# One paired input product in place of two chunks, and row scales spread by a transpose of a repeated column

## What is computed

```python
# first stack, 2 layers: four mixers side by side on one projection
for l in range(2):
    h = rms_norm(x, mix_norm_g[l])
    proj = h @ w_in[l]             # 1024 -> 2660 columns
    moba_p, mla_p, sb_p, ssm_p = split(proj, (768, 352, 768, 772))
    # mla_p: 192 columns cq, 128 ckv, 32 kr; the last 4 of ssm_p are dt
    x = x + concat(moba, mla, stick_breaking, mamba2) @ w_out[l]
    h = rms_norm(x, ffn_norm_g[l])
    u = causal_dwconv(h @ ffn_w_in[l], ffn_conv_w[l]) + ffn_conv_b[l]
    x = x + (silu(gate) * up) @ ffn_w_out[l]
# second stack, 4 layers: half a swiglu, a mixer (a, b, c, a), half a swiglu
```

## Time and profile before

| | |
|---|---|
| median of 3 runs | 2599.91 us (2598.31 to 2601.88) |
| the profiled execution | 2599.22 us, its span 2597.3 us |
| TensorE busy | 2562.4 us, 99% of the span |
| VectorE, ScalarE, GpSimd busy | 65%, 51%, 6% |
| mean granted TensorE clock | 0.998 of full |

### The profile page before, as it was taken

The page is one execution under the profiler, slowest core; times in us unless marked ns, Lnnn a source line. Parts: engine busy times, 40 slices in busy tenths (PEclk is TensorE's granted clock), DMA queues, the critical chain, the costliest instruction groups (busy, mean ns, idle before and its releaser), DMA issues.

```text
span 2597.3 us, 43244 instructions
## 1 busy us (share of the span) xinstructions
PE 2562.4 (99%) x18462; PEld 2378.8 (92%) x18462; DVE 1688.5 (65%) x2364; ACT 1322.2 (51%) x1938; POOL 156.9 (6%) x228
## 2 busy tenths in 40 slices
PE   8999999999999999999999999999999999999998
PEld 7999899998998989989988998998899899897997
DVE  6878567785665766656656665666766566566663
ACT  6756466654544554444455444444554454355542
POOL 2100011000000000000011000002000000000000
PEclk9999999999999999999999999999999999999999
DMA  7267552665766547567664766665457567563863
GB/s 223 86 175 215 170 160 84 181 193 162 209 189 200 181 134 198 184 182 195 187 218 139 198 192 178 192 190 192 147 152 198 185 179 196 191 207 99 219 186 122
DMA packets 568313, 460.26 MB, mean 177 GB/s; under 512 B 12346, under 2 KB 529290, under 8 KB 568122
## 3 DMA queue, kind: packets, MB, share of 16 engines
q1 hardware_dynamic: 562615, 441.91, 58.0%
q0 software_dynamic: 4656, 15.30, 1.8%
q10 hardware_dynamic: 851, 0.28, 0.0%
HBM read 456.37 MB, written 1.10 MB: 176 GB/s over the span
## 4 chain that ended last, share of the span: by engine, by line
PE 90%; DVE 5%; ACT 3%; DMA 1%; issue 1%; POOL 0%; DVEq 0%; POOLq 0%; SPq 0%; ACTq 0%
PE ps L899 28%; PE ps L764 16%; PE ps L766 16%; PE ps L765 16%; PE ps L718 3%; PE ps L720 3%; PE ps L719 3%; DVE wlo L1882 1%; ACT h_hi L1303 1%; DMA raw<-in_w_in 1%; PE ps L643 1%; DVE h_lo L1943 1%; ACT prob L1303 1%; ACT whi L1303 1%; PE ps L1001 1%
## 5 line engine op out<-in xcount | busy, mean ns | idle before, releaser
L1882 DVE TENSOR_TENSOR wlo<-raw,whi 128x2048 fp32r<-128x2048 f32 (+1 forms) x419 | 956.6, 2285 | 499.9 <-ACT whi L1303 499.2
L1303 ACT ACTIVATE whi<-raw 128x2048 fp32r<-128x2048 f32 (+1 forms) x421 | 802.9, 1910 | 793.2 <-DMA raw<-in_ff_w_in 420.2
L764 PE MATMUL ps<-h_hi,whi 128*128 128x256 f32 x3584 | 1006.9, 281 | 0.0
L765 PE MATMUL ps<-h_lo,whi 128*128 128x256 f32 x3584 | 1003.3, 280 | 0.0
L766 PE MATMUL ps<-h_hi,wlo 128*128 128x256 f32 x3584 | 1003.0, 280 | 0.0
L764 PEld LDWEIGHTS ps<-h_hi,whi 128*128 128x128 f32 x3584 | 673.7, 188 | 5.0 <-issue 5.0
L766 PEld LDWEIGHTS ps<-h_hi,wlo 128*128 128x128 f32 x3584 | 674.9, 188 | 0.0
L765 PEld LDWEIGHTS ps<-h_lo,whi 128*128 128x128 f32 x3584 | 673.4, 188 | 0.0
L899 PE MATMUL ps<-whi,hid_lo 128*128 128x512 f32 x880 | 296.2, 396 | 0.0
L899 PE MATMUL ps<-whi,hid_hi 128*128 128x512 f32 x880 | 295.2, 394 | 0.0
L899 PE MATMUL ps<-wlo,hid_hi 128*128 128x512 f32 x880 | 294.5, 394 | 0.0
(11 more groups left out here) (312 smaller groups left out, 2135.5 us busy)
## 6 DMA issues: line engine op xcount, KB each, us to landing
raw<-in_ff_w_in SPq DMA_DIRECT2D x176, 1024.0 KB, 6.1
raw<-in_ff_w_out SPq DMA_DIRECT2D x88, 1024.0 KB, 5.0
raw<-in_ffn_w_in SPq DMA_DIRECT2D x44, 1024.0 KB, 6.0
raw<-in_a_w_qkv SPq DMA_DIRECT2D x24, 1024.0 KB, 5.2
raw<-in_ffn_w_out SPq DMA_DIRECT2D x22, 1024.0 KB, 4.9
raw<-in_w_in SPq DMA_DIRECT2D x19, 1024.0 KB, 5.3
raw<-in_c_w_qkv SPq DMA_DIRECT2D x12, 1024.0 KB, 5.1
raw<-in_w_out SPq DMA_DIRECT2D x8, 1024.0 KB, 4.9
```

Of the source, the lines that this page charges most:

```text
L764: e.matmul(out, hi, m.h_hi[:, k, :], start=(k == 0), stop=False)
L765: e.matmul(out, hi, m.h_lo[:, k, :], start=False, stop=False)
L1303: return self.nc.scalar.activation(*a, **k)
L1882: self.e.tensor_tensor(chunk_view(m.wlo[:, slot, :], c), chunk_view(m.raw[:, slot, :], c), chunk_view(m.whi[:, slot, :], c).bitcast(F32), ...
```

## The change

It does four things.

1. The 356 columns of chunks 0 and 1 are cut into two chunks of 178, and `pair` multiplies both at once: a matmul has 356 moving columns, from two slots of the ring, and writes one bank for each `t` (banks 2 and 3). It needs both chunks before it starts and reports both done at its end. The eviction is one ScalarE instruction for each `t`.
2. Chunks 2 and 3 no longer wait for an eviction, as their banks 0 and 1 are free. In layer 0 they wait for `rows_kept`, since `turn_rows` now writes banks 0 and 1, between the two token tiles of the pair.
3. In layer 0 the first halves of both chunks are loaded and split before the start; the transfer of the four dt columns is the third on ScalarE's queue, the transfer of the tables goes behind chunk 3, and GpSimd makes `rs` before it issues its 13 transfers.
4. `spread` transposes `rs[:, t]` repeated over 128 columns, and `diagonals` is gone.

```diff
+PAIR = (QR + KVR + ROPE + 4) // 2
+IN_PIECES = ((C_CQ, [(C_CQ, PAIR)]), (C_CQ + PAIR, [(C_CQ + PAIR, PAIR - 4), (W_DT, 4)]),
...
     def spread(self):
...
-        e.wait_ge(s.diagonals, TT * r)
+        e.wait_ge(s.rstd, TT * self.rounds["norm"])
         for t in range(TT):
-            ins = e.matmul(m.ps[:, 3, t * P:(t + 1) * P], m.ones, m.diag[:, t, :], start=True, stop=True)
+            ins = e.transpose(m.ps[:, 3, t * P:(t + 1) * P], m.rs[:, t:t + 1].to_broadcast([P, P]), m.ident)
...
+    def pair(self, turn=None):
...
+        self.at(s.bank_free, self.b0)
+        if c == 0:
+            e.wait_ge(s.first_lo, 1)
+        else:
+            e.wait_ge(s.split_lo, c + 2)
+        for t in range(TT):
+            out = view(m.ps[:, 2 + t, 0:2 * PAIR], a=2)
+            for k in range(KT):
+                if k % 4 == 0:
+                    self.wait_features(2 * t + k // 4 + 1)
+                if (c, t, k) == (0, 0, 4):
+                    e.wait_ge(s.split_lo, 2)
+                if turn is not None and (t, k) == (0, 6):
+                    turn()
...
+            if t == 0:
+                ins.then_inc(s.pair_half, 1)
+                if turn is None:
+                    self.turn_rows()
+        ins.then_inc(s.chunk_done, 2)
...
+        self.paired = True
         if r == 1:
             self.begin_product()
-            chunk(0)
-            self.turn_rows()
-            chunk(1)
+            self.pair()
+            e.wait_ge(s.rows_kept, 1)
         chunk(2)
         chunk(3)
...
     def mix(self, l):
...
-        self.split(0, 0)
+        if l > 0:
+            self.split(0, 0)
         e.wait_ge(s.rstd, TT * self.rounds["norm"])
-        keep(0)
+        keep_tile(0)
+        if l == 0:
+            self.split(0, 0)
         self.split(1, 0)
-        keep(1)
-        self.split(2, 0)
+        keep_tile(1)
         e.wait_ge(s.bank_free, self.b0 + 2)
         self.act(m.c_squares, proj[:, :, C_CQ:C_KR], ACT.Square).then_inc(s.c_sq, 1)
+        self.split(2, 0)
...
     def first_norm(self, gain):
-        self.e.wait_ge(self.s.params_in, 16)
+        e, m, s, d = self.e, self.m, self.s, self.d
+        e.wait_ge(s.params_in, 16)
         for t in range(TT):
             self.rstd_x(t)
+        e.wait_ge(s.landed[1], 16 * landings(1))
+        e.dma_start(m.ext[:, 0:2 * REL + 1], d.a_rel_bias.rearrange("l h c -> (l h) c")).then_inc(s.ext_in, 16)
+        self.layer_rows(0)
```

More of the change, by code:

```diff
@@ L393 @@
     gates_ring = False
+    paired = False
     a0 = 0
@@ L539, in pick @@
             return to, of
-        for b in range(1 if l == 0 else 0, IN_CHUNKS):
+        for b in range(2 if l == 0 else 0, IN_CHUNKS):
             self.chunk(b, 0, pick)
-            if l == 0 and b == 1:
+            if l == 0 and b == 3:
                 e.dma_start(m.consts[:, CONST["upto"][0]:], d.consts[:, CONST["upto"][0]:CONST["dist"][0]]).then_inc(s.tables_in, 16)
@@ L669, in turn_rows @@
         for r in range(ROW_TILES):
-            ins = e.transpose(m.ps[:, 2 + r // 4, (r % 4) * P:(r % 4 + 1) * P], m.rows[:, r, :], m.ident)
+            ins = e.transpose(m.ps[:, r // 4, (r % 4) * P:(r % 4 + 1) * P], m.rows[:, r, :], m.ident)
         ins.then_inc(s.rows_turned, 1)
@@ L729, in tokens_chunk @@
         self.last.then_inc(self.s.chunk_done, 1)
+    def pair(self, turn=None):
+        e, m, s = self.e, self.m, self.s
+        c = self.c0
+        whi, wlo = (a[:, c % SLOTS:c % SLOTS + 2, :].rearrange("p s (k c) -> p k s c", k=KT) for a in (m.whi, m.wlo))
+        self.at(s.bank_free, self.b0)
[3 more added lines that the diff above has]
+            e.wait_ge(s.split_lo, c + 2)
+        for t in range(TT):
+            out = view(m.ps[:, 2 + t, 0:2 * PAIR], a=2)
[6 more added lines that the diff above has]
+                    turn()
+                hi, lo = m.h_hi[:, k, t * P:(t + 1) * P], m.h_lo[:, k, t * P:(t + 1) * P]
+                w_hi, w_lo = whi[:, k, :, 0:PAIR], wlo[:, k, :, 0:PAIR]
+                e.matmul(out, hi, w_hi, start=(k == 0), stop=False)
+                e.matmul(out, hi, w_lo, start=False, stop=False)
+                ins = e.matmul(out, lo, w_hi, start=False, stop=(k == KT - 1))
+            if t == 0:
[3 more added lines that the diff above has]
+        ins.then_inc(s.chunk_done, 2)
     def head(self, turn, kind):
         gates = kind in ("swiglu", "ffn1")
-        widths = IN_WIDTH[0:HEAD] if kind == "mix1" else [256] * HEAD
         self.begin_product()
+        if kind == "mix1":
+            self.pair(turn)
+            return
         for t in range(TT):
@@ L1335, in split_first @@
         m, s = self.m, self.s
-        self.e.wait_ge((s.first_landed, s.landed[0])[half], 16)
-        part = slice(1024 * half, 1024 * half + 1024)
-        self.act(m.whi[:, 0, part], m.raw[:, 0, part], ACT.Copy).then_inc((s.first_hi, s.split_hi)[half], 1)
+        if half == 0:
+            self.e.wait_ge(s.first_landed, 48)
+        else:
+            self.e.wait_ge(s.landed[0], 16)
+            self.e.wait_ge(s.landed[1], 16)
+        for b in range(2):
+            ins = self.act(first_half(m.whi, b, half), first_half(m.raw, b, half), ACT.Copy)
+        ins.then_inc((s.first_hi, s.split_hi)[half], 1 + half)
     def square_x(self, t):
@@ L1955, in first_norm @@
         self.turn_lo(1, gain)
-        for b in range(1 - AHEAD, 0):
-            self.split(b, 0)
+        self.split(2 - AHEAD, 0)
         self.e.wait_ge(self.s.rows_kept, 1)
@@ L1963, in split_first @@
         self.e.wait_ge((s.first_hi, s.split_hi)[half], 1)
-        part = slice(1024 * half, 1024 * half + 1024)
-        self.e.tensor_tensor(m.wlo[:, 0, part], m.raw[:, 0, part], m.whi[:, 0, part].bitcast(F32),
-                             ALU.subtract).then_inc((s.first_lo, s.split_lo)[half], 1)
+        for b in range(2):
+            ins = self.e.tensor_tensor(first_half(m.wlo, b, half), first_half(m.raw, b, half), first_half(m.whi, b, half).bitcast(F32),
+                                       ALU.subtract)
+        ins.then_inc((s.first_lo, s.split_lo)[half], 1 + half)
     def weigh_sum(self, t, half, weight):
@@ L2913, in landings, with first_half @@
 def landings(c):
-    return sum(2 if k in NARROW else 1 for k in range(c % SLOTS, c + 1, SLOTS))
+    return sum(2 if k > 1 and k in NARROW and k - 1 in NARROW else 1 for k in range(c % SLOTS, c + 1, SLOTS))
+def first_half(a, b, half):
+    return a[:, b, :].rearrange("p (k c) -> p k c", k=KT)[:, 4 * half:4 * half + 4, 0:PAIR]
 def chunk_view(ap, c):
```

60 lines of the change are left out of this document (26 added, 34 removed).

## The result

| | before | after |
|---|---|---|
| median of the runs | 2599.86 us (8 runs, 2598.31 to 2601.88) | 2608.61 us (8 runs, 2605.38 to 2610.40) |
| profiled execution, its span | 2599.22, 2597.3 | 2605.38, 2603.5 |

The ratio is 1.0031, with an interval of 1.0021 to 1.0040: the change costs 8.7 us.

The account below looks back on a forecast made before the run. TensorE is busy 99% of the span, but chunk 5's arrival sets layer 0's time. Gains of 1.5 (layer 0), 0.8 (layer 1) and 2.4 (`spread`) sum to 4.7 us, giving 2595.2; range 2590.5 to 2601.

Parts of the forecast that it names:

- Price of a matmul: Mixers' input product: one 356-column matmul takes 0.163 us in place of a pair's 0.230, saving 3.2 us of TensorE per layer.
- Layer 1: 0.8 us: Layer 1's input product: wait in the pair 1.2 us, stand of 1.8 before `cn`, gain 0.8 of the 3.2 us.
- the bound with the fallen clock: Layer 1: a loss of 1.3 us if the clock falls after its stand as after the longer one.
- Layer 0, start: Start of layer 0: larger first loads, small dt pieces and splits move the first matmul from 10.19 to 13.0.
- Layer 0, chunk 5: Layer 0's weight transfer: slot freed at 23.0, landing at 29.6, transposes of `cn` at 37.4.
- second rival: Layer 0: GpSimd's 13 transfers meet chunks 4 and 5; with the old 15.57 us, landing 38.6, time 2604.2; chance 0.1.
- Layer 0, TensorE: Before layer 0's `cn`: TensorE arrives at 34.3, stands 3.1 us, loses 2.1 to low clock; layer 0 gains 1.5.
- The clock: TensorE behind layer 0's stand: a 2.4 us stand lowered the clock, 1.45 did not, so 2.1 us is counted.
- `spread`: 2.4 us: In 11 places two transposes of 0.22 us replace four passes of 0.44, a 2.4 us gain; lost VectorE work counts nothing.

Follow-up runs that it names:

- experiment 2: The changed kernel with the pair only in layers after the first; layer 0's start, loads and order as before, on chunks of 178 columns: 2604.34 us.
- experiment 4: The changed kernel without the transfer of the four dt columns in 1024 small pieces, loading 178 neighbouring columns in layer 0: 2606.29 us.
- experiment 5: The changed kernel, with GpSimd waiting for chunk 5 ahead of the `up` weights and last rows, and no longer for chunk 3 between them: 2602.59 us.
- 7: The kernel before with only the new `spread`, each of its two transposes issued twice (four passes): 2602.80 us.
- experiment 1: The kernel before with only the new `spread`: two transposes of the repeated column in 11 places, no diagonal matrix: 2603.41 us, ratio 1.0019.
- 9: The kernel before with the new `spread`'s two transposes, but VectorE's diagonals still made and waited for: 2604.93 us.
- experiment 10: The kernel before with only the new `spread`, plus one extra matmul at chunk 11 of the hidden product in each `swiglu` stage: 2602.02 us.
- 3: The changed kernel, with chunk 5 split behind the chain that makes `cn` on ScalarE and VectorE, and chunk 2 evicted before it: 2602.54 us.
- 6: The changed kernel with the old `spread` (diagonal matrices, two float32 matmuls), so the pair alone: 2606.51 us.

## Why the prediction was wrong

Said: 2595.2. Came: 2608.6, outside the range. By its own steps:

- **Price of a matmul.** Said 0.163 for 356 columns, measured 0.167. Right.
- **Layer 1: 0.8 us.** Came 0.7, with a wait in the pair of 1.0 (said 1.2) and a stand of 1.7 (said 1.8). Right in mechanism and size; experiment 2 shows that the bound with the fallen clock can be met.
- **Layer 0, start.** Said 13.0 for the first matmul, came 14.94. The step priced the 1024 small pieces at 1.2 us, from a microsecond in which 845 small packets passed alone; experiment 4 measures them at 3.2. The term was mis-sized, and it moved the end of the pair from 23.0 to about 25.2.
- **Layer 0, chunk 5.** This is the step that failed. Said: landing at 29.6, from a queue that stays full behind 13.4 us. It did not stay full. Everything issued early had landed by about 23.6, and chunk 5 could not leave until 25.30, so its time was its own 5.35 us (experiment 5) plus what GpSimd's transfers took, and they had moved to exactly this place: 11.29. I had written that they "start late and leave the queue to the weights"; they left it to chunks 2 to 4, which nobody waited for, and met chunk 5. That is the second rival ("Chunk 5 is no faster than before"), to which I gave 0.1: landing 36.6 against its 34.3 to 38.6. By that rival's own formula this landing gives 2602.2; what is missing to 2608.6 is the drift and the distance of the median from the profile, both below.
- **Layer 0, TensorE.** Stand 7.8 where I said 3.1; the clock fell behind it, 2.3 us where I said 2.1. Together layer 0 lost 5.66 where I had a gain of 1.5.
- **The clock.** That it falls behind a stand of 3 us was read off two stands of before, and the runs do not bear out that the length decides. Ahead of `cn` in layer 0 the clock fell with stands of 2.24 us (experiment 2) and 2.37 (7), and held with 2.32 (1) and 2.35 (9). In experiment 10 it fell while TensorE was busy, 1.6 us before its stand for the eviction of chunk 0. That the cost came near (2.3 for 2.1) says nothing for the rule, as the stand was 7.8 us and not 3.1. What decides between holding and falling is open. The Trainium skill's rule that I weighed ("TensorE: Matmul & The Clock Gate", section "HAM oscillation — how this bites in real kernels": gaps in which TensorE waits for data bring its clock to half) agrees with the stands of 7.8, 3.2 and 2.56 us; behind those of 1.71, 2.32 and 2.35 us the granted clock stayed at 1.00. Experiment 1, the matmul behind the stand and the stretch from it on; then experiment 10, two stretches ahead of the stand and the matmul behind it:

```profile
40.68 0.33 PE L1079 MATMUL ps<-consts,xn 128*128 128x128 f32 x1 [2.32 <-DVE xn L2454]
40.68:45.00 4.32, 4.32 (x37) 4.32 (x38) 4.18 (x8) 4.00 (x7) 0.00 (x0) 1.00 0.54 187
```

```profile
20.00:21.80 1.80, 1.80 (x19) 1.80 (x17) 1.71 (x1) 0.06 (x1) 1.66 (x3) 0.99 1.00 335
21.80:23.39 1.59, 1.59 (x8) 1.42 (x7) 0.58 (x1) 1.16 (x1) 1.42 (x3) 0.50 0.97 297
25.11 0.55 PE L718 MATMUL ps<-whi,h_hi 128*128 128x256 f32 x1 [1.72 <-ACT proj L1308]
```

- **`spread`: 2.4 us.** The places gave 2.5, and the step stopped there. That two passes fewer change the rate at which the 19 chunks behind run was in none of my terms or rivals; I put it at nothing without a reason, and with it the part costs 4.2 us (experiment 1). This is the second step that failed. The rate of 5.71 is in no row of before, but its trace already had two rates, seven stages at 5.65 and one at 5.62, and a gain of 0.22 stood ahead of 912 matmuls, where 1% more on each is 1.0.

The median lies 3.2 us above the profiled execution of after. Three more stages at 5.71 would do it (five of the eight were not at it in that profile, and experiments 1, 2, 3 and 5 show five or six that are), but the slower executions have no trace, so this is argued and not shown. A stand with a fallen clock in a later mixer, as in the profile of 6 (4.4 us), would do it too.

Open is what sets the rate. The steps of matmuls repeat every six, and the first ones behind the `spread` already differ; that is all that the traces show. The Trainium skill says in "TensorE: Matmul & The Clock Gate", section "Architectural detail: the array is 16× 32×32, not 1× 128×128", that TensorE's queue may pull weight loads ahead of matmuls in flight; whether that is what locks in differently, no run here shows.

## What to carry to other kernels

Before a transfer is moved later, ask what its issue waits for and what is in the queue at that moment, not how full the queue is on average: a full queue ahead of it hides the wait for its slot, an empty one doesn't. Where a chain of small results stands behind a large piece of work that it does not need, in two engines' queues, move it ahead first; a saving on TensorE ahead of such a chain is easily lost (here the pair in layer 1 cost 0.9 us with the chain behind chunk 5, and gained 2.6 by the profiles with the chain ahead). And when a change of a few passes stands ahead of a long run of equal matmuls, compare the period of that run in both traces: 1% of it was more than four times the gain.

## What the hardware showed that I had not expected

- A run of equal matmuls (128 x 256, float32r) on TensorE ran here at one of three steady rates at the full granted clock: 5.62, 5.65 and 5.71 us for 48 of them. It kept the one in which it entered, over 912 matmuls, and one matmul more moved it from 5.71 to 5.65 in mid-run, in five stages of five.
- 1024 pieces of 16 bytes, in one transfer beside others, delayed the first matmul by 3.2 us, nearly three times the 1.2 us that I had worked out from a microsecond of 845 packets.
- The same 1 MB load took 5.35 us without GpSimd's 1.2 MB beside it, and 11.29 and 12.03 with it.
- The length of a stand alone did not tell whether the granted clock falls: in one place it held at 2.32 and 2.35 us and fell at 2.24 and 2.37, and once it fell 1.6 us before TensorE stood.
